# A recurrent layer in twelve tiles of 128 channels in place of sixteen of 96

## The reference

```python
D_RNN = 3 * D_MODEL // 2          # 1536
N_RNN_BLOCKS = 16                 # of RNN_BLOCK_W = 96 channels
...
    z = h @ w_in                                   # 1024 x 3072
    xr, gate = jnp.split(z, 2, axis=-1)
    xr = centred_depthwise_conv(xr, conv_w, conv_b)    # 4 taps
    y = (rg_lru(xr, w_a[0], b_a[0], w_x[0], b_x[0], lam[0], reverse=False)
         + rg_lru(xr, w_a[1], b_a[1], w_x[1], b_x[1], lam[1], reverse=True))
    y = y.astype(h.dtype) * jax.nn.gelu(gate)
    return y @ w_out                               # 1536 x 1024
```

## Time and profile before

| what | value |
|---|---|
| median of 3 runs | 1435.37 us (1433.19 to 1438.77) |
| profiled execution, its span | 1433.6 us |
| PE busy | 1333.0 us (93%) |
| DVE busy | 1046.3 us (73%) |
| ACT busy | 719.5 us (50%) |
| DMA, mean over the span | 218 GB/s |
| recurrent stage (first z matmul to first matmul of the norm behind it) | 362.68 to 567.23 us |

### The profile page before, as it was taken

The page is one execution under the profiler, slowest core; times in us unless marked ns, Lnnn a source line. Parts: engine busy times, 40 slices in busy tenths (PEclk is TensorE's granted clock), DMA queues, the critical chain, the costliest instruction groups (busy, mean ns, idle before and its releaser), DMA issues.

```text
span 1433.6 us, 20178 instructions
## 1 busy us (share of the span) xinstructions
PE 1333.0 (93%) x7892; PEld 1179.6 (82%) x7892; DVE 1046.3 (73%) x1508; ACT 719.5 (50%) x971; POOL 0.4 (0%) x5
## 2 busy tenths in 40 slices
PE   6989799999999997899997899999899999999986
PEld 6778699999777776799996679998878887878875
DVE  5666687776787788677776756866467869678685
ACT  3432445453565656354443544433356657567563
POOL 0000000000000000000000000000000000000000
PEclk9969899999999998999999899999899999999998
DMA  8729687876587775676663252221065978878772
GB/s 330 270 81 342 204 316 255 304 244 230 184 284 253 263 257 202 239 248 224 232 219 120 97 191 74 90 87 41 1 249 201 367 245 309 287 270 322 244 258 94
DMA packets 84351, 312.90 MB, mean 218 GB/s; under 512 B 9505, under 2 KB 9729, under 8 KB 83521
## 3 DMA queue, kind: packets, MB, share of 16 engines
q1 hardware_dynamic: 82080, 298.88, 58.9%
q10 hardware_dynamic: 2176, 12.74, 2.6%
HBM read 310.54 MB, written 1.05 MB: 217 GB/s over the span
## 4 chain that ended last, share of the span: by engine, by line
PE 80%; DVE 11%; ACT 4%; DMA 3%; issue 2%; SPq 0%; DVEq 0%; ACTq 0%
PE ps L451 79%; DVE w_low L410 3%; DMA ring<-stream 2%; DVE junk L410 1%; ACT w_high L410 1%; DMA ring<-moe 1%; DVE rs L410 1%; DVE x L410 1%; PE ps L1071 1%; DVE y_experts L410 1%; DVE sc L410 0%; DVE t_one L410 0%; DVE sm L410 0%; ACT L410 0%; ACT t_two L410 0%
## 5 line engine op out<-in xcount | busy, mean ns | idle before, releaser
L410 DVE TENSOR_TENSOR w_low<-ring,w_high 128x1024 fp32r<-128x1024 f32 x368 | 441.7, 1221 | 161.0 <-ACT w_high L410 156.7
L410 ACT ACTIVATE w_high<-ring 128x1024 fp32r<-128x1024 f32 x368 | 385.8, 1058 | 290.5 <-PE ps L451 195.1
L451 PE MATMUL ps<-x_high,w_high 128*128 128x256 f32 (+1 forms) x784 | 235.1, 300 | 27.5 <-DVE x_low L410 20.8
L451 PE MATMUL ps<-x_low,w_high 128*128 128x256 f32 (+1 forms) x784 | 232.3, 296 | 0.0
L451 PE MATMUL ps<-x_high,w_low 128*128 128x256 f32 (+1 forms) x784 | 232.2, 296 | 0.0
L410 DVE CUSTOM_DVE_ANT_0 junk<-ring,cond 128x1024 f32<-128x1024 f32 x137 | 166.9, 1221 | 31.9 <-DMA ring<-stream 23.3
L451 PEld LDWEIGHTS ps<-x_high,w_high 128*128 128x128 f32 x784 | 154.0, 196 | 36.7 <-issue 12.7
L451 PEld LDWEIGHTS ps<-x_low,w_high 128*128 128x128 f32 x784 | 153.9, 196 | 2.5
L451 PEld LDWEIGHTS ps<-x_high,w_low 128*128 128x128 f32 x784 | 153.6, 196 | 2.8
L451 PE MATMUL ps<-h_high,w_high 128*128 128x256 f32 x512 | 145.4, 284 | 1.7 <-DVE h_low L410 1.0
L451 PE MATMUL ps<-h_low,w_high 128*128 128x256 f32 x512 | 144.9, 283 | 0.0
(11 more groups left out here) (315 smaller groups left out, 2019.0 us busy)
## 6 DMA issues: line engine op xcount, KB each, us to landing
ring<-stream SPq DMA_DIRECT2D x376, 512.0 KB, 4.8
ring<-moe SPq DMA_DIRECT2D x192, 512.0 KB, 4.9
tab_two<-tab ACTq DMA_DIRECT2D x1, 2824.0 KB, 13.3
gw<-gw ACTq DMA_DIRECT2D x1, 2304.0 KB, 15.5
cond<-cvec ACTq DMA_DIRECT2D x2, 512.0 KB, 5.5
x<-xT ACTq DMA_DIRECT2D x1, 1024.0 KB, 11.6
ctx_first<-ctxT ACTq DMA_DIRECT2D x1, 1024.0 KB, 5.6
ctx<-ctxT ACTq DMA_DIRECT2D x1, 1024.0 KB, 4.7
```

Source lines behind the costliest of these rows:

```text
L410: return op(*a, **k).then_inc(self.sem, 1)
L451: return pe.matmul(out, stationary, moving, start=start, stop=stop, skip_group_check=True)
```

## The change

The 1536 channels are laid out in twelve tiles of 128. Every four blocks of 96 form a group g of three tiles. Tile i of a group holds the whole block i on 96 partitions, and on the remaining 32 (32i to 32i+31) a third of the group's fourth block; a third of 96 channels is a quarter of the tile, hence the name `QUAD`. Weights, parameters and the output matrix are permuted accordingly before the launch.

The gates of a tile's own block are a 128x128 product whose rows and columns for the foreign 32 channels are zero. For the fourth block ACT copies the 32 rows of each of three convolved tiles into one gathered tile `xb_three` of 96 rows (`shared_rows`), PE multiplies that with the 96x96 blocks (`shared_gates`), and ACT takes the tanh of it in 32-row slices back into the places of the three tiles, over the values that the own product left there.

The rest of the stage moves with it. The order of the pieces is now all z pieces, then all output pieces. DVE's second half works on groups of three tiles (1536 elements a row) except in the last group, where it goes tile by tile. The exp and the second tanh (`decays`) come for a whole group behind its gates. The modulation products keep their number, 24 calls, but are dealt out by `RNN_CHUNKS`. Three XP buffers replace two, nine XCV buffers four, and these lie in the area of `w_low`. The gates' weights grow from 96x6144 to 128x7680 floats; they are loaded at the same place in ACT's program.

```diff
+BW = 96
+NT, NGR, QUAD = 12, 4, 32
+TILES = [(g, i) for g in range(NGR) for i in range(3)]
...
-W_QKV, W_ATT, W_MLP0, W_RNN, W_MLP1, W_IN2, W_OUT2, W_MOE, W_END = 0, 12, 20, 84, 132, 196, 224, 232, 424
+W_QKV, W_ATT, W_MLP0, W_RNN, W_MLP1, W_IN2, W_OUT2, W_MOE, W_END = 0, 12, 20, 84, 120, 184, 212, 220, 412
...
-RNN_SEQ = [("z", b, j) for b in range(2) for j in range(2)]
-for _b in range(NB):
-    RNN_SEQ += [("z", _b + 2, j) for j in range(2) if _b + 2 < NB] + [("o", _b - 3, 0)] * (_b >= 3)
-RNN_SEQ += [("o", b, 0) for b in range(NB - 3, NB)]
+RNN_SEQ = [("z", t, j) for t in range(NT) for j in range(2)] + [("o", t, 0) for t in range(NT)]
...
-TWO_CHUNKS = (1, 3, 5, 7, 9, 11, 13, 15)
+RNN_CHUNKS = {("z", t): 2 if t < 8 else 1 for t in range(2, NT)} | {("o", t): 1 for t in (0, 1, 2, 3, 5, 6, 9, 10)}
...
+    for t in range(2, NT):
+        order += "ww" + "aa" * RNN_CHUNKS.get(("z", t), 0)
+    for t in range(NT):
+        order += "w" + "aa" * RNN_CHUNKS.get(("o", t), 0)
...
+        self.GT, self.Y = pbt("gt", aB, NT), pbt("y", aT1, NT)
+        self.TA, self.AA, self.TI = pgidt("ta", aB + 3072), pgidt("aa", aB + 6144), pgidt("ti", aX + 2048)
+        self.HSC = view("hsc", aXL + 1024, 1536).rearrange("p (i d t) -> p i d t", i=3, d=2)
+        self.XCV = pbt("xcv", aWL, 9)
+        self.XP = view("xp", aWL + 2304, 780).rearrange("p (a t) -> p a t", a=3)
+        self.XB3 = view("xb_three", aWL + 3084, 512, BW).rearrange("p (g t) -> p g t", g=2)
...
+    def z_half(t, j):
+        if t >= 2 and j == 0:
+            pe.wait_ge(s.gt, t - 1)
+        piece = whole(RNN_AT["z", t, j])
+        for k in range(KT):
+            ins = mm(PS[:, t % 2, j * 256:(j + 1) * 256], piece[:, k * P:(k + 1) * P], m.XF[:, k, :], k == 0, k == KT - 1)
+        ins.then_inc(s.used, 1)
+    def first_z():
+        pieces = [whole(RNN_AT["z", 0, j]) for j in range(2)]
+        for k in range(KT):
+            if k % 2 == 0:
+                pe.wait_ge(s.x_whole, k // 2 + 1)
+            for j in range(2):
+                ins = mm(PS[:, 0, j * 256:(j + 1) * 256], pieces[j][:, k * P:(k + 1) * P], m.XF[:, k, :], k == 0 and j == 0, k == KT - 1)
+                if k == KT - 1:
+                    ins.then_inc(s.used, 1)
+    def z_of(t):
+        z_half(t, 0)
+        z_half(t, 1)
+    def gate_half(unit, d, p, weights, x):
+        if unit >= 1:
+            pe.wait_ge(s.gate_ps, 2 * (unit - 1) + d + 1)
+        for n in range(2):
+            ins = mm(PS[0:p, 2 + d, n * 256:(n + 1) * 256], weights[:, 2 * d + n, :], x, True, True)
+        ins.then_inc(s.gate_mm, 1)
+    def own_gates(t):
+        if t == 0:
             pe.wait_ge(s.in_gw, 16)
+        pe.wait_ge(s.xcv, t + 1)
         for d in range(2):
+            gate_half(own_unit(t), d, P, m.GWO[:, t, :, :], m.XCV[:, t % 9, :])
+    def shared_gates(g):
+        pe.wait_ge(s.xb, 3 * g + 3)
+        for d in range(2):
+            gate_half(shared_unit(g), d, BW, m.GWB[:, g, :, :], m.XB3[:, g % 2, :])
+    def out_of(t):
+        piece = whole(RNN_AT["o", t, 0])
+        pe.wait_ge(s.y_gated, t // 3 + 1 if t < NT - 3 else t - NT + 7)
         for k in range(KT):
+            if t == NT - 1 and k in (2, 4, 6):
                 ins.then_inc(s.sums, 1)
+            ins = mm(PS[:, 4 + k // 2, (k % 2) * 256:(k % 2 + 1) * 256], piece[:, k * P:(k + 1) * P], m.Y[:, t, :], t == 0 and k % 2 == 0, False)
         ins.then_inc(s.used, 1)
+    first_z()
     z_of(1)
+    z_of(2)
+    for g in range(3):
+        z_half(3 * g + 3, 0)
+        own_gates(3 * g)
+        z_half(3 * g + 3, 1)
+        own_gates(3 * g + 1)
+        z_half(3 * g + 4, 0)
+        own_gates(3 * g + 2)
+        z_half(3 * g + 4, 1)
+        shared_gates(g)
+        z_of(3 * g + 5)
+    for i in range(3):
+        out_of(i)
+        own_gates(9 + i)
+    shared_gates(3)
+    for t in range(3, NT):
+        out_of(t)
...
+    def z_of(t):
+        act.wait_ge(s.used, RNN_AT["z", t, 1] + 1)
+        if t >= 3:
+            act.wait_ge(s.xcv, t - 2)
+        A(m.XP[:, t % 3, 2:258], PS[:, t % 2, 0:256], ACT.Copy, apart=True)
+        A(m.GT[:, t, :], PS[:, t % 2, 256:512], ACT.Copy, s.gt, apart=True)
+    def shared_rows(t):
+        rows = slice(QUAD * (t % 3), QUAD * (t % 3 + 1))
+        act.wait_ge(s.xcv, t + 1)
+        A(m.XB3[rows, (t // 3) % 2, :], m.XCV[rows, t % 9, :], ACT.Copy, s.xb, apart=True)
+    def own_gates(t):
+        g, i = t // 3, t % 3
+        if g >= 2 and i == 0:
+            act.wait_ge(s.scan, g - 1)
+            col = NT * d + t
+            act.wait_ge(s.gate_mm, 2 * own_unit(t) + d + 1)
+            A(m.TA[:, g % 2, i, d, :], PS[:, 2 + d, 0:256], ACT.Tanh, scale=0.5, bias=m.hba[:, col:col + 1], apart=True)
+            A(m.TI[:, g % 2, i, d, :], PS[:, 2 + d, 256:512], ACT.Tanh, s.gate_ps, scale=0.5, bias=m.hbx[:, col:col + 1], apart=True)
+    def shared_gates(g):
+        for d in range(2):
+            act.wait_ge(s.gate_mm, 2 * shared_unit(g) + d + 1)
+            for i in range(3):
+                col, rows = NT * d + 3 * g + i, slice(QUAD * i, QUAD * (i + 1))
+                A(m.TA[rows, g % 2, i, d, :], PS[rows, 2 + d, 0:256], ACT.Tanh, scale=0.5, bias=m.hba[rows, col:col + 1], apart=d > 0 or i > 0)
+                A(m.TI[rows, g % 2, i, d, :], PS[rows, 2 + d, 256:512], ACT.Tanh, s.gate_ps if i == 2 else None, scale=0.5, bias=m.hbx[rows, col:col + 1], apart=True)
+    def decays(t):
+        g, i = t // 3, t % 3
+        for d in range(2):
+            col = NT * d + t
+            A(m.AA[:, g % 2, i, d, :], m.TA[:, g % 2, i, d, :], ACT.Exp, s.gates if d else None, scale=m.cs2[:, col:col + 1], bias=m.cs2[:, col:col + 1], apart=d > 0)
+        for d in range(2):
+            col = NT * d + t
+            A(m.TA[:, g % 2, i, d, :], m.TA[:, g % 2, i, d, :], ACT.Tanh, scale=m.cs[:, col:col + 1], bias=m.cs[:, col:col + 1], apart="two")
+    def inputs_scale(g):
+        A(m.TA[:, g % 2, :, :, :], m.TA[:, g % 2, :, :, :], ACT.Sqrt, s.tl, scale=0.25)
+    def gate_gelu(lo, hi):
+        A(m.GT[:, lo:hi, :], m.GT[:, lo:hi, :], ACT.Gelu_apprx_tanh, s.gelu, apart=True)
+    shared_rows(0)
+    z_of(2)
+    shared_rows(1)
+    for g in range(3):
+        own_gates(3 * g)
+        shared_rows(3 * g + 2)
+        z_of(3 * g + 3)
+        own_gates(3 * g + 1)
+        if g > 0:
+            inputs_scale(g - 1)
+            gate_gelu(3 * g - 3, 3 * g)
+        own_gates(3 * g + 2)
+        z_of(3 * g + 4)
+        shared_rows(3 * g + 3)
+        shared_gates(g)
+        decays(3 * g)
+        z_of(3 * g + 5)
+        shared_rows(3 * g + 4)
+        decays(3 * g + 1)
+        decays(3 * g + 2)
+    own_gates(9)
+    shared_rows(11)
+    own_gates(10)
+    inputs_scale(2)
+    gate_gelu(6, 12)
+    own_gates(11)
+    shared_gates(3)
+    for t in range(9, 12):
+        decays(t)
+    inputs_scale(3)
...
+    def chunks(*at):
+        for _ in range(sum(RNN_CHUNKS[key] for key in at)):
+    def scan_inputs(g):
+        W2, AA = (ap[:, g % 2, :, :, :].rearrange("p i d t -> p (i d t)") for ap in (m.TI, m.AA))
+        for i in range(3):
+            t = 3 * g + i
+            vv.wait_ge(s.gates, t + 1)
+            op(vv.scalar_tensor_tensor, m.TI[:, g % 2, i, :, :], m.TI[:, g % 2, i, :, :], 1.0, m.XCV[:, t % 9, :].unsqueeze(1).broadcast_to([P, 2, S]), ALU.add, ALU.mult, apart=True)
+    def scans(g, i, last):
+        for d in range(2):
+            at = slice(None, None, -1 if d else 1)
+            op(vv.tensor_tensor_scan, m.HSC[:, i, d, at], m.AA[:, g % 2, i, d, at], m.TI[:, g % 2, i, d, at], 0.0, ALU.mult, ALU.add,
+               inc=s.scan if d and last else None, apart=i > 0 or d > 0)
+    def group(g):
+        scan_inputs(g)
+        W2, TL = (ap[:, g % 2, :, :, :].rearrange("p i d t -> p (i d t)") for ap in (m.TI, m.TA))
+        vv.wait_ge(s.tl, g + 1)
+        op(vv.tensor_tensor, W2, W2, TL, ALU.mult)
+        for i in range(3):
+            scans(g, i, i == 2)
+        if g == 0:
+        tiles = slice(3 * g, 3 * g + 3)
+        op(vv.tensor_tensor, m.Y[:, tiles, :], m.HSC[:, :, 0, :], m.HSC[:, :, 1, :], ALU.add)
+        vv.wait_ge(s.gelu, g + 1)
+        op(vv.tensor_tensor, m.Y[:, tiles, :], m.Y[:, tiles, :], m.GT[:, tiles, :], ALU.mult, inc=s.y_gated)
+    def last_group():
+        scan_inputs(3)
+        vv.wait_ge(s.tl, 4)
+        for i in range(3):
+            t = 9 + i
+            W2 = m.TI[:, 1, i, :, :]
+            op(vv.tensor_tensor, W2, W2, m.TA[:, 1, i, :, :], ALU.mult)
+            for d in range(2):
+                at = slice(None, None, -1 if d else 1)
+                op(vv.tensor_tensor_scan, m.HSC[:, i, d, at], m.AA[:, 1, i, d, at], m.TI[:, 1, i, d, at], 0.0, ALU.mult, ALU.add, apart=d > 0)
+            op(vv.tensor_tensor, m.Y[:, t, :], m.HSC[:, i, 0, :], m.HSC[:, i, 1, :], ALU.add)
+            op(vv.tensor_tensor, m.Y[:, t, :], m.Y[:, t, :], m.GT[:, t, :], ALU.mult, inc=s.y_gated)
+    convolved(0)
+    convolved(1)
+    for t in range(2, 7):
+        chunks(("z", t))
```

(55 more changed lines are left out.)

156 lines of the change are left out of this document (33 added, 123 removed).

## The result

| | median | range | runs |
|---|---|---|---|
| before | 1434.38 us | 1433.19 to 1438.77 | 4 |
| after | 1419.85 us | 1417.52 to 1423.08 | 4 |

The account below looks back on a forecast made before the run. PE work plus a tail of waits bounds the recurrent stage. Reaching the norm 31.8 us earlier, less 3.2 for slow clock and 2 for `gw`, gives 26.6: from 1435.4 to 1409 us, own range 1402 to 1418, 8-in-10 1395 to 1424.

Parts of the forecast that it names:

- a ring that paces tiles 2 to 7: Rival, 12%: 36 pieces for z tiles 2 to 7 arrive at 2.06 us each, 19 us more, giving 1425.
- PE work: Recurrent stage: matmuls fall from 448 to 352 at 0.432 us each, 193.5 to 152.1 us, removing 41.4.
- PE's waits, tile by tile: Recurrent stage in the new order: PE waits for ring pieces and ACT, 10.2 us in all; last output ends at 525.0.
- more than 20 us of waits in the stage: Sign against the forecast: it is wrong if PE waits more than 20 us in the recurrent stage.
- a rival of 7%: Clock rival, 7%: each of the three longer PE waits in the stage brings 1.2 GHz, 3.15 us each, giving 1418.
- What is late next: Stage end: DVE's six `junk` products and the weight split delay `x`; norm 31.8 us earlier, 10.4 of PE's gain returned.
- Costs elsewhere: Outside the stage: `gw` load grows from 2.36 to 3.93 MB, costing 0 to 6.2 us, taken as 2.
- Table loads: ACT in the recurrent stage: 11 table loads instead of 25, 1.28 us each; the removal saves nothing by itself.
- The rule weighed in the prediction: Rival, 3%: each ACT table switch adds a drain of about 1380 ns, about 4 us on the sum, giving 1413.
- "The other stages have the same instructions.": Outside the recurrent stage: the other stages' instructions are the same; no cost was charged for them.
- the lock of DVE and PE: Rival, slower than before, 4%: SP's order locks DVE and PE, ring pieces cost 2.44 us, giving 1445; decides from 2.35.
- The waits were not covered: Rival, waits covered, 15%: stage waits of 2.1, 3.3 and 2.7 us shrink to 4 in all, giving 1398.

Follow-up runs that it names:

- `warm`: 18 extra 256-column matmuls with unread results in three PE waits of the changed kernel: 1416.08 us; nine in two waits, atop three other changes: 1394.33 us.

## Why the prediction was right, and where its size was off

The sign and the 8-in-10 range, 1395 to 1424, held; the gain was forecast 12 us too large. The time, 1419.85, lies outside the range of my own forecast, 1402 to 1418. It lies in the wide one because that one was stretched for a ring that paces tiles 2 to 7, which did not happen; that it covers the two losses below is luck. In profiles the forecast of 26.6 becomes 11.8 like this: 8.1 are missing in the stage up to the norm's first matmul (180.8 instead of 172.7), 0.8 come back since the lower clock behind it cost 2.4 instead of 3.2, 0.3 more is lost ahead of the stage (2.3 instead of 2, and not where the 2 were charged), and 7.2 are lost behind the norm. 26.6 - 8.1 + 0.8 - 0.3 - 7.2 = 11.8.

- **PE work.** Right: 704 records, 379 ns for each shape at full clock, and 352 x 0.432 = 152.1.
- **PE's waits, tile by tile.** Right in place and sum: 0.5, 2.1, 3.3, 2.7 and the ring's small ones forecast, 10.2 together; 2.64, 4.42, 2.16 and 0.72 measured, 9.9. Outputs 6 and 9 did not wait for `y`, as forecast. The sign "more than 20 us of waits in the stage" was badly drawn: with the wait for `x` the forecast itself has 20.6, and 21.2 were measured.
- **The clock behind them.** This is the step that was too small in the stage. I charged the lower clock once, in the tail, and left the waits inside the stage to a rival of 7%, at 3.15 us each. That rival had the mechanism: each of the three waits did lower the clock, but for 1.7 us each, as the runs with `warm` show; its 1418 comes near the time partly by luck, since its price was too high and it lacked the loss in the experts. The earlier trace rows held one wait, of 6.53, and that had cost the clock; that waits of 2 to 4 us don't was an assumption without a row. 169.6 - 152.1 - 9.9 leaves 7.6 us: 5.2 are these, 2.4 are spread over the rest and were not followed.
- **What is late next.** Right: 10.4 forecast between the last output and the norm, 11.3 waited, behind six `junk` and four `w_low` by name. The `w_high` wait for their DMA, as the argument with the ring slots had it.
- **Costs elsewhere: the load of `gw`.** Two us were charged for 1.57 MB more, and nothing was measured. While it ran PE was 9.86 busy in 10, as before (9.85), and it landed 14.0 us after its issue (15.5 before). From this issue to the first z it takes 197.5 us, against 197.9 before. The stage starts 2.3 us later in after, but that was lost ahead of the load; over the profiles of all kernels with the same load it starts anything from 1.6 earlier to 2.5 later (361.11 to 365.15, against 362.68).
- **Table loads.** 11, as forecast, and inside the stage PE waited for ACT only once, at the last gathered product. The rule weighed in the prediction can be read directly:

```profile
492.20 1.28 ACT L424 ACT_TABLE_LOAD   x1
493.49 1.48 ACT L424 ACTIVATE ta<-ta 128x1536 f32<-128x1536 f32 x1
```

The successor starts 1.29 us behind the load's start. The Trainium skill, ScalarE: Activation LUTs, What ACT_TABLE_LOAD costs, has a drain of about 1380 ns besides; here the measurement decides, and that rival is out.
- **"The other stages have the same instructions."** This sentence failed, and it is the largest single miss behind the stage: 5.9 of 7.2 us. The instructions are the same; the places of their operands are not, and with the old place the 5.9 are gone. The diff has it in plain sight, in the line of `RPAR`, and I read that line as bookkeeping. Of the remaining 1.3, 1.0 lie between the norm and the experts; the 14 profiles scatter there by up to 4 us between the second MLP and the experts, and this was not followed.
- **The rivals.** The ring does not pace tiles 2 to 7, as this stretch of after shows:

```profile
388.00:414.00 26.00, 25.76 (x119) 21.93 (x118) 15.84 (x29) 14.45 (x35) 0.00 (x0) 1.00 0.91 341
```

It moves 341 GB/s at a share of 0.91, that is 0.524/(341/0.91) = 1.40 us a piece (1.46 forecast), and PE is busy 25.76 of 26. With that the lock of DVE and PE is out too, which wanted 2.35 a piece. The waits were not covered (9.9 us of them stand in the trace), and the time does not follow the filled part of the array (379 ns for 128x128 and for 96x96).

## What to carry to other kernels

Here a wait of 2 to 4 us on PE had to be booked at its length plus 1.7 us of lower clock, and before one removes it, one reads which engine stands right behind it: taking away the ACT wait brought a DVE wait of 3.58. When a change resizes a buffer, look at what is placed behind it, and compare the distance between like matmuls in a stage that was not touched; here 160 bytes cost 6 us, and the total time, which scatters by as much, did not show it. When work on the main engine shrinks, the other engines' order at the stage's end wants a new look: the sum that the norm reads belonged ahead of the last two products and of the four `w_low`.
